# Differential attention in a float32 kernel: keys stacked high over low, banks waited for one by one, low parts on GpSimd

## The reference

```python
s = jnp.einsum('bqhcd,bkhcd->bhcqk', q, k).astype(jnp.float32) * (DIFF_QK_DIM ** -0.5)
p = jax.nn.softmax(s, axis=-1)
pd = (p[:, :, 0] - lam * p[:, :, 1]).astype(v.dtype)
return jnp.einsum('bhqk,bkhd->bqhd', pd, v)
```

## Time and profile before

| | us |
|---|---|
| median of 3 runs (lowest, highest) | 3786.72 (3783.73, 3791.21) |
| the profiled execution | 3786.28 |
| its span | 3784.5 |
| TensorE busy | 3434.4 (91%) |
| VectorE busy | 1929.6 (51%) |
| ScalarE busy | 1177.6 (31%) |
| GpSimd busy | 421.5 (11%) |
| chain that ended last: TensorE, VectorE, ScalarE | 77%, 12%, 7% |

### The profile page before, as it was taken

One profiled execution on the slowest core, in us unless ns is written; L12 is line 12 of the kernel. 1 busy time (PEld: TensorE's weight loads), 2 busy tenths in 40 slices (PEclk: granted clock), 3 DMA queues, 4 the chain that ended last, 5 costly groups with the idle time before them and its releaser, 6 DMA issues.

```text
span 3784.5 us, 38279 instructions
## 1 busy us (share of the span) xinstructions
PE 3434.4 (91%) x15655; PEld 2844.4 (75%) x15655; DVE 1929.6 (51%) x2742; ACT 1177.6 (31%) x1713; POOL 421.5 (11%) x295
## 2 busy tenths in 40 slices
PE   3999888797999999959979999999896799999997
PEld 2888676676888888847768888887785678888886
DVE  5624465656554444573554343446495653333334
ACT  5311455525221111243241111224445441111222
POOL 4000222221000000120200000003092000000000
PEclk9999788888999999969889999999897899999999
DMA  5434100020333222101111111120111111111121
GB/s 186 143 122 145 37 20 31 19 94 20 98 100 100 89 89 84 56 30 32 30 56 45 45 45 45 48 64 24 45 46 56 56 45 45 45 45 45 50 62 45
DMA packets 187943, 234.81 MB, mean 62 GB/s; under 512 B 8887, under 2 KB 148138, under 8 KB 187770
## 3 DMA queue, kind: packets, MB, share of 16 engines
q1 hardware_dynamic: 177146, 194.73, 16.5%
q0 software_dynamic: 9184, 32.41, 2.3%
q10 hardware_dynamic: 1440, 5.24, 0.4%
HBM read 215.52 MB, written 16.83 MB: 61 GB/s over the span
## 4 chain that ended last, share of the span: by engine, by line
PE 77%; DVE 12%; ACT 7%; issue 3%; DMA 1%; POOL 0%; DVEq 0%; SPq 0%; ACTq 0%; POOLq 0%
PE psum L470 25%; PE psum L472 24%; PE psum L471 24%; DVE small L594 2%; ACT temp L777 2%; ACT U_hi L476 1%; DVE H L1265 1%; DVE small L1167 1%; ACT prob L1142 1%; DVE split L481 1%; PE psum L1073 1%; ACT split L476 1%; DVE U_lo L481 1%; PE psum L767 1%; DVE small L619 1%
## 5 line engine op out<-in xcount | busy, mean ns | idle before, releaser
L470 PE MATMUL psum<-U_hi,split 128*128 128x512 f32 x2108 | 835.0, 396 | 61.9 <-DVE split L481 37.6
L471 PE MATMUL psum<-U_lo,split 128*128 128x512 f32 x2108 | 829.0, 393 | 0.0
L472 PE MATMUL psum<-U_hi,split 128*128 128x512 f32 x2108 | 828.1, 393 | 0.0
L476 ACT CAST split<-raw 128x1024 fp32r<-128x1024 f32 (+1 forms) x277 | 282.6, 1040 | 1298.4 <-PE psum L472 918.4
L470 PE MATMUL psum<-split,A_hi 128*128 128x512 f32 x1536 | 599.5, 390 | 3.5 <-ACT temp L777 3.5
L472 PE MATMUL psum<-split,A_lo 128*128 128x512 f32 x1536 | 598.7, 390 | 0.0
L471 PE MATMUL psum<-split,A_hi 128*128 128x512 f32 x1536 | 598.6, 390 | 0.0
L1265 DVE TENSOR_TENSOR H<-H,psum 128x512 f32<-128x512 f32 x416 | 281.4, 686 | 590.0 <-PE psum L472 590.0
L470 PEld LDWEIGHTS psum<-U_hi,split 128*128 128x128 f32 x2108 | 401.2, 190 | 153.5 <-DVE split L481 38.8
L481 DVE TENSOR_TENSOR split<-raw,split 128x1024 fp32r<-128x1024 f32 (+1 forms) x277 | 343.3, 1255 | 296.2 <-ACT split L476 296.0
L472 PEld LDWEIGHTS psum<-U_hi,split 128*128 128x128 f32 x2108 | 401.0, 190 | 84.7
(11 more groups left out here) (302 smaller groups left out, 4079.5 us busy)
## 6 DMA issues: line engine op xcount, KB each, us to landing
raw<-in_mlp_w_dram SPq DMA_DIRECT2D x128, 512.0 KB, 4.4
raw<-in_ada_w_dram SPq DMA_DIRECT2D x96, 512.0 KB, 4.3
raw<-in_w_in_dram SPq DMA_DIRECT2D x38, 512.0 KB, 3.9
raw<-in_w_up_dram SPq DMA_DIRECT2D x32, 512.0 KB, 4.0
raw<-in_w_down_dram SPq DMA_DIRECT2D x32, 512.0 KB, 4.4
H<-in_x_dram ACTq DMA_DIRECT2D x8, 512.0 KB, 4.4
raw<-in_w_out_mix_dram SPq DMA_DIRECT2D x8, 512.0 KB, 3.6
H<-in_x_dram POOLq DMA_DIRECT2D x8, 512.0 KB, 6.7
```

The source lines that it names most:

```text
L470: pe.matmul(out, l_hi, r_hi, start=start, stop=False)
L471: pe.matmul(out, l_hi, r_lo, start=False, stop=False)
L472: return pe.matmul(out, l_lo, r_hi, start=False, stop=stop)
L476: return act.copy(hi, src).then_inc(*k.hi.inc(*key))
```

## The change

Keys: for each component a tile `KK` holds the high part in partitions 0 to 63 and the low part in 64 to 127; queries `Q_hi`, `Q_lo` hold the same 64 channels in both halves. One matmul of `Q_hi` with `KK` gives high x high and high x low, a second with `Q_lo` gives low x high and low x low. The loads fetch the 64 channels twice (`twice`), 24 units instead of 16. `KK` and `V` exist twice, for alternate heads, in the split slots' place; `O` moves into free parts of `U_lo`.

Banks 0, 1, 2 (and 3, 4) are taken one at a time. The score scale goes into the queries when they leave PSUM, so the maximum is negated by its own instruction; both components share one row of small values, with one reciprocal.

Low parts of attention's units are made by GpSimd (`low_att_unit`), behind its addition, and have a semaphore of their own. The next head's units are split in steps 1 to 5 and, its second query half, in its own first step. Projection units are split in steps 27, 32, 33. In the output projection the transposes of a half's four heads stand together ahead of tile 2 and of tile 4.

The diff, cut to its core:

```diff
+        self.KK = [place(f"KK{i}", split_at + i * 20 * KB, [P, 2, KEYS], F32R) for i in range(2)]
+        self.V = [place(f"V{i}", split_at + i * 20 * KB + 10 * KB, [P, 2, KEYS], F32R) for i in range(2)]
+
+        self.Q_hi = place("Q_hi", r_at, [P, 2, T], F32R)
+        self.Q_lo = place("Q_lo", r_at + 8 * KB, [P, 2, T], F32R)
+        self.O = [place(f"O{i}", u_at + (8 + 16 * i) * KB, [P, TPC, HEADS * P]) for i in range(NCH)]
...
+        def twice(dram, h, c, first, n, at):
+
+            return [(lambda r, e=e: r[64 * e:64 * e + 64, at:at + n], dram[h, 64 * c:64 * c + 64, first:first + n])
+                    for e in range(2)]
...
-            both = lambda what, h: [(what, h, c) for c in range(NCH)]
-            units.append(Unit([(lambda r: r[:], self.d_q[h])], after=both("q", h)))
-            units.append(Unit([(lambda r: r[:], self.d_k[h])], after=both("k", h)))
+            if h == 0:
+                queries(h)
+            for c in range(2):
+                units.append(Unit(twice(self.d_k, h, c, 0, T, 0), after=both("k", h), att=("k", h, c)))
...
+            units.append(Unit(twice(self.d_kc, h, 0, 0, CTX, 0) + twice(self.d_kc, h, 1, 0, CTX, CTX) +
+                              [(lambda r: r[:, 512:768].rearrange("p (k n) -> p k n", k=2), v[:, TT:TT + CTT, :])],
+                              after=[("kc", h), ("v", TT), ("v", TT + 1)], att=("x", h, 0)))
             units.append(Unit([(lambda r: r[:].rearrange("p (k n) -> p k n", k=TT), v[:, 0:TT, :])],
-                              after=[("v", t) for t in range(TT)]))
+                              after=[("v", t) for t in range(TT)], att=("v", h, 0)))
+            if h:
+                queries(h)
...
+ATT_IN_PROJECT = {7: [("q", 0, 0)], 8: [("q", 0, 1), ("k", 0, 0)], 9: [("k", 0, 1)], 10: [("x", 0, 0), ("v", 0, 0)]}
...
-            act_weights(k, act, on, 17 + m)
+            if m < 7:
+                act_weights(k, act, on, k.first["conv"] + 5 + m)
+            for key in ATT_IN_PROJECT.get(m, ()):
+                act_att_unit(k, act, on, k.att[key])
...
+    for m in range(12):
+        for key in ATT_IN_PROJECT.get(m, ()):
+            low_att_unit(k, pool, on, k.att[key])
...
+def act_att_unit(k, act, on, u):
+
+    what, h, i = u.att
+    KK, V = k.KK[h % 2], k.V[h % 2]
+    on.wait_ge(*k.landed(u))
+    for s_before in u.before:
+        on.wait_ge(*k.free_slot(s_before))
+    if what == "q":
...
+        last = act.copy(k.Q_hi[:, :, i * CH:(i + 1) * CH], u.raw[:].rearrange("p (c n) -> p c n", c=2))
+    elif what == "k":
+        last = act.copy(KK[:, i, 0:T], u.raw[:])
+    elif what == "x":
+        act.copy(KK[:, :, T:KEYS], u.raw[:, 0:2 * CTX].rearrange("p (c n) -> p c n", c=2))
+        last = act.copy(V[:, 0, T:KEYS], u.raw[:, 2 * CTX:3 * CTX])
+    else:
+        last = act.copy(V[:, 0, 0:T], u.raw[:])
...
+    on.wait_ge(*k.hi.at("w", u.s))
+    on.wait_ge(*k.att_lo.now())
+    on.wait_ge(*k.pool_done.now())
+    if what == "q":
+        s = slice(i * CH, (i + 1) * CH)
+        last = engine.tensor_tensor(k.Q_lo[:, :, s], u.raw[:].rearrange("p (c n) -> p c n", c=2),
+                                    k.Q_hi[:, :, s].bitcast(F32), ALU.subtract)
+    elif what == "k":
+        last = engine.tensor_tensor(KK[low, i, 0:T], u.raw[low, :], KK[low, i, 0:T].bitcast(F32), ALU.subtract)
...
+    else:
+        last = engine.tensor_tensor(V[:, 1, 0:T], u.raw[:], V[:, 0, 0:T].bitcast(F32), ALU.subtract)
+    last.then_inc(*k.att_lo.inc("w", u.s))
...
+def pe_scores(k, pe, h, qt, c, first, n, at):
...
-    return three_passes(pe, out, u.hi[s, qt * P:(qt + 1) * P], u.lo[s, qt * P:(qt + 1) * P], src.hi[s, first:first + n],
-                        src.lo[s, first:first + n], True, True)
+    keys = k.KK[h % 2][:, c, first:first + n]
+    s = slice(qt * P, (qt + 1) * P)
+    pe.matmul(out, k.Q_hi[:, c, s], keys, start=True, stop=False)
+    return pe.matmul(out, k.Q_lo[:, c, s], keys, start=False, stop=True)
...
-                for u in units(h)[:3]:
-                    on.wait_ge(*k.lo.at("w", u.s))
-            for b in range(3):
-                k.banks.take(on, ("scores", i, b), *([(k.exp_done, (0, i))] if b < 2 else
-                                                    [(k.exp_done, (0, i)), (k.exp_done, (1, i))]), slot=b)
-            pe_scores(k, pe, h, qt, 0, False, 0, 0)
-            pe_scores(k, pe, h, qt, 0, False, 512, 512)
-            pe_scores(k, pe, h, qt, 0, True, 0, 1024).then_inc(*k.pe_done.inc("first", i))
+                for key in (("q", h, 0), ("k", h, 0), ("k", h, 1), ("x", h, 0)):
+                    on.wait_ge(*k.att_lo.at("w", k.att[key].s))
+            elif qt == TPC:
+                on.wait_ge(*k.att_lo.at("w", k.att["q", h, 1].s))
+            k.banks.take(on, ("scores", i, 0), (k.exp_done, (0, i)), slot=0)
+            pe_scores(k, pe, h, qt, 0, 0, CH, 0)
+            k.banks.take(on, ("scores", i, 1), (k.exp_done, (0, i)), slot=1)
+            pe_scores(k, pe, h, qt, 0, CH, CH, CH)
+            k.banks.take(on, ("scores", i, 2), (k.exp_done, (0, i)), (k.exp_done, (1, i)), slot=2)
+            pe_scores(k, pe, h, qt, 0, T, CTX, T).then_inc(*k.pe_done.inc("first", i))
             on.wait_ge(*k.pe_done.at("first", i))
-            pe_scores(k, pe, h, qt, 1, True, 0, 1280).then_inc(*k.pe_done.inc("scores", 0, i))
+            pe_scores(k, pe, h, qt, 1, T, CTX, KEYS).then_inc(*k.pe_done.inc("scores", 0, i))
...
-            for b in (3, 4):
-                k.banks.take(on, ("scores", i, b), (k.exp_done, (1, i)), slot=b)
-            pe_scores(k, pe, h, qt, 1, False, 0, 1536)
-            pe_scores(k, pe, h, qt, 1, False, 512, 2048).then_inc(*k.pe_done.inc("scores", 1, i))
-            if qt == TT - 1:
-                for u in units(h)[:2]:
-                    k.freed[u.s] = k.pe_done, ("scores", 1, i)
+            k.banks.take(on, ("scores", i, 3), (k.exp_done, (1, i)), slot=3)
+            pe_scores(k, pe, h, qt, 1, 0, CH, KEYS + CTX)
+            k.banks.take(on, ("scores", i, 4), (k.exp_done, (1, i)), slot=4)
+            pe_scores(k, pe, h, qt, 1, CH, CH, KEYS + CTX + CH).then_inc(*k.pe_done.inc("scores", 1, i))
+            k.freed[k.att["q", h, qt // TPC].s] = k.pe_done, ("scores", 1, i)
+            for c in range(2):
+                k.freed[k.att["k", h, c].s] = k.pe_done, ("scores", 1, i)
...
-            uc, uv = units(h)[2:]
-            on.wait_ge(*k.lo.at("w", uv.s))
+            for key in (("x", h, 0), ("v", h, 0)):
+                on.wait_ge(*k.att_lo.at("w", k.att[key].s))
...
-def weights_at_step(i):
-
-    if i % TT == TT - 1 and i < len(STEPS):
-        at = 24 + 4 * (i // TT) + 5
-        return (at, at + 1)
-    if i % TT == 1 and i > TT:
-        at = 24 + 4 * ((i - 2) // TT) + 7
-        return (at, at + 1)
-    return ()
+def units_at_step(i):
+
+    h, qt = i // TT + 1, i % TT
+    if qt == 0 and 1 <= i // TT < HEADS:
+        return [("q", i // TT, 1)]
+    if h >= HEADS:
+        return []
+    return {1: [("k", h, 0)], 2: [("k", h, 1)], 3: [("x", h, 0)], 4: [("v", h, 0)], 5: [("q", h, 0)]}.get(qt, [])
+
+
+WEIGHTS_AT_STEP = {27: (0, 1), 32: (2,), 33: (3, 4)}
...
-        for s in weights_at_step(i):
-            act_weights(k, act, on, s)
+        for key in units_at_step(i):
+            act_att_unit(k, act, on, k.att[key])
+        for n in WEIGHTS_AT_STEP.get(i, ()):
+            act_weights(k, act, on, k.first["mix"] + n)
...
-        dve.tensor_reduce(sm[:, 0:1], score_columns(k, c), AX_X, ALU.max).then_inc(*k.step.inc())
-        on.wait_ge(*k.step.now())
-        dve.tensor_scalar(sm[:, 1:2], sm[:, 0:1], -SCALE, None, ALU.mult).then_inc(*k.measured.inc("max", c, i))
+        dve.tensor_reduce(sm[:, c:c + 1], score_columns(k, c), AX_X, ALU.max, negate=True).then_inc(
+            *k.measured.inc("max", c, i))
...
-            dve.reciprocal(sm1[:, 3:4], sm1[:, 2:3]).then_inc(*k.step.inc())
-            dve.reciprocal(sm0[:, 3:4], sm0[:, 2:3]).then_inc(*k.scaled.inc("sum", i))
-            on.wait_ge(*k.step.now())
-            dve.scalar_tensor_tensor(sm1[:, 4:5], sm1[:, 3:4], sm0[:, 2:3], k.lam[:, 4:5], ALU.mult,
+            dve.reciprocal(sm[:, 4:6], sm[:, 2:4]).then_inc(*k.scaled.inc("sum", i))
+            on.wait_ge(*k.scaled.at("sum", i))
+            dve.scalar_tensor_tensor(sm[:, 6:7], sm[:, 5:6], sm[:, 2:3], k.lam[:, 4:5], ALU.mult,
                                      ALU.mult).then_inc(*k.scaled.inc("coefficient", i))
...
-    for i in range(len(STEPS)):
-        p0, p1 = k.prob0[i % 3], k.prob1[i % 2]
-        on.wait_ge(*k.act_done.at("p1", i))
-        pool.tensor_tensor(p0[:, 0:T], p0[:, 0:T], p1[:, CTX:KEYS], ALU.add)
-        pool.tensor_tensor(p0[:, T:KEYS], p0[:, T:KEYS], p1[:, 0:CTX], ALU.add).then_inc(*k.pool_done.inc("mix", i))
+    for i in range(len(STEPS) + 1):
+        if i:
+            p0, p1 = k.prob0[(i - 1) % 3], k.prob1[(i - 1) % 2]
+            on.wait_ge(*k.att_lo.now())
+            on.wait_ge(*k.act_done.at("p1", i - 1))
```

(16 more changed lines are left out.)

160 lines of the change are left out of this document (96 added, 64 removed).

## The result

The changed kernel takes **3703.4 us** (median of 4 runs, 3699.88 to 3708.53) against 3788.97 us for the kernel before beside it (4 runs, 3783.73 to 3792.22): ratio 0.9781, 95% interval 0.9762 to 0.9799. The forecast was 3730 with a range of 3706 to 3764. The direction held, and so did most terms, but the time lies 2.6 us under the range. The profiled execution took 3704.34 us with a span of 3702.5, so it is 81.9 us faster than the profiled one before.

A forecast was written before the change was run, and what follows sets the result against it. In the attention loop no engine is full; a chain round all of them decides. Savings of 51.6 (loop) + 1.4 (ahead) + 5.6 - 1.1 (behind) = 57.5 us gave 3729, written 3730, range 3706 to 3764.

The forecast's parts named there:

- steps 0 to 2: Attention loop's first three steps, at half clock: 33.9 us before, 26.3 after, the third about 9.5 with TensorE full.
- plain step at full clock: Attention loop: 7.95 us instead of 9.30, ScalarE deciding up to the first exponential (3.44), then 3.09 and 1.42.
- half clock in steps 3 to 30, beyond 28 plain steps: Attention loop: 28 steps at a mean of 8.71 us, 243.9 in all, against 7.95 at full clock.
- unit casts and squares: Attention loop: 18 more unit casts on ScalarE, 6.0 us; squares of the output in the last head, 6 x 0.45 = 2.7.
- step 27, beyond a plain one: Attention loop: two output-projection units gated, cast and split there delay ScalarE's scaling from 0.93 to 7.9, 7.0 us.
- last read to the first projection matmul: Stretch after the attention loop: 17 us instead of 22.6, so 5.6 less, as the pair of units is gone.
- behind: Output projection: four head transposes ahead of tile 2 make it wait for VectorE's first addition, 1.1 us more.
- so I keep 29%: Attention loop after the first steps: half-clock share stays 29%, since TensorE idles 13% against 15%; mean step 8.71 us.
- Rival C: Attention loop: clock stays at half, every step 11.4 us, 75 more, 3804, slower than before; chance 0.05.
- Rival A: Attention loop: transposes wait for GpSimd, 0.8 to 1.0 us more in 18 steps, 3747; chance 0.08.
- Rival B: Attention loop: component 1's four matmuls fall behind the second exponential, 0.5 us more in 28 steps, 3743; chance 0.12.
- Loads of 64 partitions: Key and query loads, fetched twice: bounded by 4 and 8 us, asked for 16 us ahead, hidden, costed at nothing.

The follow-up runs named there:

- e2: The kernel before, with each score matmul contracting over all 128 partitions instead of 64, same number, width and order of instructions: 3753.98 us, ratio 0.9912.
- e3: The kernel before, with banks 0, 1 and 2 waited for one by one, so component 1's first six score matmuls run early: 3747.46 us, ratio 0.9894.
- e10: The kernel before, with both score matmuls over 128 partitions and banks 0 to 2 waited for one by one: 3728.54 us, ratio 0.9832.
- e1: The changed kernel, with score matmuls over partitions 0 to 63 only, products with the low keys left out: 3712.67 us, ratio 0.9801.
- e4: The changed kernel, with banks 0 to 2 waited for together, so component 1's score matmuls stand behind the second exponential: 3722.36 us, ratio 0.9828.
- e6: The changed kernel, with the scaling of component 2 moved from ScalarE to GpSimd, ahead of its additions: 3725.49 us, ratio 0.9831.
- e8: The changed kernel, with the maximum's sign changed by a VectorE instruction of its own, twice a step: 3713.45 us, ratio 0.9796.
- e11: e7 with 384 of 1280 columns of component 2's scaling on GpSimd, and the first two units' gates, casts and low parts at other steps: 3686.66 us, ratio 0.9726.
- e7: The changed kernel, with five units' gate multiplications on GpSimd ahead of their casts, the first two's low parts there too, casts in steps 26 and 28: 3692.32 us.
- e5: The changed kernel, with the attention units' low parts on VectorE instead of GpSimd: 3710.31 us, ratio 0.9796.

## Why the prediction was right or wrong

The sum, term by term (us):

| term | predicted | measured |
|---|---|---|
| up to the first exponential | 1.4 less | 2.4 less |
| steps 0 to 2 | 26.3 | 24.4 |
| plain step at full clock | 7.95 | 7.96 to 7.98 |
| half clock in steps 3 to 30, beyond 28 plain steps | 21.3 | 1.5 at most |
| unit casts and squares | 8.7 | 5.1 |
| step 27, beyond a plain one | 7.0 | 7.2 |
| last read to the first projection matmul | 17 | 18.1 |
| behind | 1.1 more | 1.3 more |

**The step that failed** is "so I keep 29%", the share of time at half clock, which made 8.71 us of a 7.95-us step. It is worth 21.3 us in 28 steps; measured were 1.5, all in step 28, its squares (0.25) with them. That 19.8 is most of the 24.5 us between the forecast saving (57.5) and the measured one (82.0); unit casts and squares are 3.6, steps 0 to 2 1.9 (the third was taken at half clock, 9.5, and ran at full clock, 8.04), the start 1.0, and 1.8 go the other way (tail 1.1, behind 0.2, step 27 0.2, plain steps of 7.96 0.3). I read the share from TensorE's idle time alone, 13% against 15%, and the idle share came out no smaller than before (1.34 of 7.96 us, 17%, against 1.31 of 9.31, 14%), so by that reading nothing should have changed. The prediction counted that a matmul over 128 rows costs the time of one over 64, which is true of the single matmul (0.40 us), and stopped there. e2 shows what that missed: with 128 rows, instructions and order unchanged, half clock in the stage goes from 146.8 to 47.8 us. e3 shows the second part: with the idle stretch of 1.25 us taken out of each plain step, at 64 rows, it is 99.0. With both (e10) every plain step away from a stall is at full clock. e1 and e4 undo one each, and falls come back in both, but few. Either edit alone removes a good part of the half clock, and the changed kernel has both.

**The range's lower end failed with it.** The text had the right number, "with no half clock after the start the sum is 21 less (3708)", and the low end of 3706 left nothing for the other terms, which were off by 4.7 more in sum. The measured median is 3703.4.

**Rival C** had the clock stay at half. The opposite happened in plain steps. Its last sentence did come true: the stall in step 27 is followed by a fall (0.58, then 0.50). The Trainium skill (TensorE: Matmul & The Clock Gate, "The HAM clock gate") was cited for activity as what releases the throttle; in e2, with as many matmuls as before, TensorE is busy for less of a plain step (7.64 against 7.99 us) and the clock is up all the same, and no run here shows what counts as activity. Both halves of the rule were weighed on idle time alone.

**Rival A** did not occur: additions 2.40, low parts 2.39 us. e6 shows where it would have begun: with 3.52 us more on GpSimd transposes wait for it (20.4 us from 440 to 600).

**Rival B** did not occur: component 1's four matmuls run at 519.12 to 520.2, ahead of the exponential's end.

**The plain step** came out by the right chain. The maximum starts at +1.16 (1.2 predicted), the first exponential at +3.49 (3.44). e8 confirms that the negation was in the chain (0.18 a step for the one place that the sum counted at 0.17, ahead of the second exponential; ahead of the first ScalarE covers it), and e11 that ScalarE bounds the stretch up to the first. What the prediction did not ask is what the removed score matmuls are worth once ScalarE decides: at full clock nothing (e10 beside e8).

**Unit casts** were costed at 0.3 in a plain step and 0.8 beside a cast of the convolution, and cost 0.08 and 0.6: ScalarE's 0.74 us wait for the coefficient takes most, and the cast itself holds the engine only 0.94 (537.05 to 537.99). Squares cost 0.25 instead of 0.45. **Step 27** was priced right, and e7 shows it was avoidable; TensorE stood still 8.15 us (8 predicted).

**Loads of 64 partitions** appear in no wait of the loop, as assumed. Ahead of it ScalarE waited 6.1 and 1.4 us for the first head's two query loads (casts at 339.34 and 341.83), over 50 us before they are wanted at 395. Moving the low parts to GpSimd is worth 6.1 us of the loop (e5). The stalls at the heads' starts are not cured by that engine but by splitting the units one a step ahead of need: they are gone in e5 too, where VectorE makes the low parts.

What stays open: which property of a stretch makes the clock fall. The runs show that 64-row score matmuls and idle time both act, not how they are combined, nor why some steps of e1 and e4 see a fall and their like do not. Going from 64 rows to 128 also takes away short pauses between matmuls (below), and no run has the one without the other. In e3 and e4 the longest idle stretch and the idle share move together.

## What to carry to other kernels

Before carrying a clock share over a change, ask whether the change alters how much of the array each matmul uses and how its idle time is cut; packing two 64-row passes into one of 128 rows paid here through the clock, while the matmuls it removed gave a plain step nothing, since ScalarE set its length. If the share is uncertain, let the range run past the all-full-clock end, not up to it. Work that waits on another engine's product belongs a step away from it: the same two gates cost 7.2 us inside step 27 and next to nothing a step or more ahead on an engine with room (e7 changes place and engine together, so the shares of the two are not shown); and a move to that engine should be sized by its own row, since its scaling took 2.6 times ScalarE's.

## What was not expected of the hardware

- Score matmuls over 64 rows and over 128 take the same time at the same clock (0.39 and 0.40 us for 512 columns in e1 and in the changed kernel), but the 64-row kernel spends three times as long at half clock (146.8 against 47.8 us, before and e2).
- Where TensorE goes from 64-row matmuls to 128-row ones or back, the next starts later: the first transpose 0.20 us after the start of the last 256-column score matmul before and 0.12 in e2, the first score matmul 0.20 after that of the last transpose before and 0.03 in e2. In a plain step TensorE is busy 0.35 us longer for it (before and e2), 0.52 in e1 beside the changed kernel.
- GpSimd's multiplication by a per-partition value is dearer per element than its two-input addition: 3.52 us for 1280 columns, against 2.40 for 1024 (and 1.28 for 384). The same scaling takes 1.37 on ScalarE.
- GpSimd is as slow on 64 partitions as on 128 (2380 and 2389 ns at 1024 columns).
- In e6 VectorE's tiny coefficient operation (128x1, 220 ns in the changed kernel) started beside one of GpSimd's additions in 18 of 32 steps and then ended as an addition ended, after 0.29 to 2.03 us; in the other 14 it took 0.22. One of them:

```profile
522.05 0.16 DVE L1292 RECIPROCAL small<-small 128x2 f32<-128x2 f32 x1
522.25 1.39 DVE L1294 SCALAR_TENSOR_TENSOR small<-small,lam 128x1 f32<-128x1 f32 x1
```

The addition on GpSimd ran from 521.26 to 523.62, and the operation on VectorE, started at 522.25, ended at 523.64; the reciprocal ahead of it was not slowed.
